# Expert weights as one 8 KB run per partition, with the turned operands taken in steps of two

## What is computed

```python
def _ec_moe(h, w_r, w_g, w_u, w_d):
    ...
    gate, idx = lax.top_k(aff.T, cap)
    xe = t[idx]
    hid = jax.nn.silu(jnp.einsum('ecd,edf->ecf', xe, w_g)) * jnp.einsum('ecd,edf->ecf', xe, w_u)
    ye = jnp.einsum('ecf,efd->ecd', hid, w_d) * gate[..., None].astype(t.dtype)
    out = jnp.zeros_like(t).at[idx.reshape(-1)].add(ye.reshape(-1, d))
```

## Time and profile before

| what | value |
|---|---|
| median of 3 runs | 2408.3 us (2407.99 to 2409.02) |
| span of the profiled execution | 2406.4 us |
| PE busy | 2205.8 us (92%) |
| PE weight loads busy | 1677.9 us (70%) |
| DVE busy | 1613.7 us (67%) |
| ACT busy | 1261.6 us (52%) |
| POOL busy | 545.4 us (23%) |
| DMA | 520.40 MB, 169530 packets |

### The profile page before, as it was taken

One profiled execution on the slowest core, in us unless ns is written; L12 is line 12 of the kernel. 1 busy time (PEld: TensorE's weight loads), 2 busy tenths in 40 slices (PEclk: granted clock), 3 DMA queues, 4 the chain that ended last, 5 costly groups with the idle time before them and its releaser, 6 DMA issues. The chain is left out here.

```text
span 2406.4 us, 32340 instructions
## 1 busy us (share of the span) xinstructions
PE 2205.8 (92%) x11028; PEld 1677.9 (70%) x11028; DVE 1613.7 (67%) x1832; ACT 1261.6 (52%) x1486; POOL 545.4 (23%) x430
## 2 busy tenths in 40 slices
PE   8899998969999999977899999969969999999993
PEld 5677776747777777746788888757756777777772
DVE  3566664578888888855566566552258888888883
ACT  3444443157777777743443434341107777777772
POOL 1100000012234233205232222200000332344222
PEclk9999998979999999987999999989979999999997
DMA  7000004769999999934111112152169999999983
GB/s 264 1 14 8 13 14 156 280 228 378 385 385 378 396 382 383 351 95 135 36 49 49 49 48 61 56 191 88 70 245 342 382 381 389 390 380 383 393 295 126
DMA packets 169530, 520.40 MB, mean 216 GB/s; under 512 B 11808, under 2 KB 49440, under 8 KB 169184
## 3 DMA queue, kind: packets, MB, share of 16 engines
q1 hardware_dynamic: 162272, 494.05, 54.4%
q0 software_dynamic: 7168, 25.17, 4.5%
HBM read 481.43 MB, written 37.75 MB: 216 GB/s over the span
## 5 line engine op out<-in xcount | busy, mean ns | idle before, releaser
L1764 DVE TENSOR_TENSOR m_w_lo<-s_raw,m_w_hi 128x2048 fp32r<-128x2048 f32 x384 | 865.9, 2288 | 144.6 <-ACT m_w_hi L1713 143.0
L1713 ACT ACTIVATE m_w_hi<-s_raw 128x2048 fp32r<-128x2048 f32 x384 | 731.1, 1916 | 175.9 <-PE m_ps_down L1809 77.3
L1807 PE MATMUL m_ps_gate<-m_w_hi,m_xeT_hi 128*96 128x512 f32 x512 | 206.0, 402 | 3.8 <-DVE m_xeT_lo L1770 3.8
L1807 PE MATMUL m_ps_down<-m_w_hi,m_hidT_hi 128*96 128x512 f32 x512 | 203.9, 398 | 3.8 <-DVE m_hidT_lo L1770 3.8
L1809 PE MATMUL m_ps_gate<-m_w_hi,m_xeT_lo 128*96 128x512 f32 x512 | 204.3, 399 | 0.0
L1809 PE MATMUL m_ps_down<-m_w_hi,m_hidT_lo 128*96 128x512 f32 x512 | 204.1, 399 | 0.0
L1807 PE MATMUL m_ps_up<-m_w_hi,m_xeT_hi 128*96 128x512 f32 x512 | 203.9, 398 | 0.0
L1684 POOL DMA_INDIRECT acc<-m_ye,m_row_scatter x32 | 47.0, 1469 | 688.4 <-ACT m_ye L1730 688.4
L1809 PE MATMUL m_ps_up<-m_w_hi,m_xeT_lo 128*96 128x512 f32 x512 | 202.7, 396 | 0.0
L1808 PE MATMUL m_ps_gate<-m_w_lo,m_xeT_hi 128*96 128x512 f32 x512 | 202.5, 395 | 0.0
L1808 PE MATMUL m_ps_down<-m_w_lo,m_hidT_hi 128*96 128x512 f32 x512 | 202.3, 395 | 0.0
(11 more groups left out here) (228 smaller groups left out, 4200.4 us busy)
## 6 DMA issues: line engine op xcount, KB each, us to landing
s_raw<-in_w_gate SPq DMA_DIRECT2D x128, 1024.0 KB, 7.6
s_raw<-in_w_up SPq DMA_DIRECT2D x128, 1024.0 KB, 7.3
s_raw<-in_w_down SPq DMA_DIRECT2D x128, 1024.0 KB, 7.8
s_raw<-in_w_qkv_b SPq DMA_DIRECT2D x16, 512.0 KB, 5.8
s_raw<-in_w_qkv_b SPq DMA_DIRECT2D x32, 256.0 KB, 6.1
s_raw<-in_w_o_b SPq DMA_DIRECT2D x1, 8192.0 KB, 23.2
acc<-o_x SPq DMA_DIRECT2D x12, 512.0 KB, 2.6
xn<-o_xn SPq DMA_DIRECT2D x12, 512.0 KB, 3.0
```

Of the source, the lines that this page charges most:

```text
L1713: act.activation(hi[:, split, :, :].rearrange("p k n -> p (k n)"), raw[:, slot, :], ACT.Copy).then_inc(hi_ready, 1)
L1764: dve.tensor_tensor(lo[:, split, :, :].rearrange("p k n -> p (k n)"), raw[:, slot, :], hi[:, split, :, :].rearrange("p k n -> p (k n)"), A ...
L1807: pe.matmul(out[:, cols], left_hi[:, k, :], hi[:, split, kk, cols], start=(k == 0), stop=False)
```

## The change

The loads read two neighbouring matrix rows into one partition: partition p of piece j now holds rows 256j+2p and 256j+2p+1, which are one run of 8 KB in HBM and in the slot. So that the products still sum over the same rows, each transpose takes its 128 columns in steps of two: block k = 2j+kk of the turned operand holds the columns 256j+2p+kk.

```diff
             def load(e, matrix, j, first_slot):
-                src = matrix[layer].rearrange("e (c k p) n -> e c p k n", c=4, p=P)[bass.ds(e, 1), j]
-                sp.dma_start(raw[:, first_slot + j, :].rearrange("p (k n) -> p k n", k=2),
-                             src.rearrange("e p k n -> (e p) k n")).then_inc(shared.landed[first_slot + j], 16)
+                src = matrix[layer].rearrange("e (c p k) n -> e c p (k n)", c=4, p=P)[bass.ds(e, 1), j]
+                sp.dma_start(raw[:, first_slot + j, :],
+                             src.rearrange("e p n -> (e p) n")).then_inc(shared.landed[first_slot + j], 16)
...
                 wait(pe, T_lo, n)
+                rows = src.rearrange("t (c p k) -> t c k p", c=4, k=2)
                 for k in range(KD):
-                    last = pe.transpose(T_ps[:, k, 0:CAP], src[:, k * P:(k + 1) * P], shared.ident[0:CAP, 0:CAP])
+                    last = pe.transpose(T_ps[:, k, 0:CAP], rows[:, k // 2, k % 2, :], shared.ident[0:CAP, 0:CAP])
...
-        src = matrix[layer, 0].rearrange("(c k p) n -> c p k n", c=4, p=P)
-        sp.dma_start(self.raw[:, first_slot + j, :].rearrange("p (k n) -> p k n", k=2),
-                     src[j]).then_inc(self.landed[first_slot + j], 16)
+        src = matrix[layer, 0].rearrange("(c p k) n -> c p (k n)", c=4, p=P)
+        sp.dma_start(self.raw[:, first_slot + j, :], src[j]).then_inc(self.landed[first_slot + j], 16)
```

## The result

| kernel | median, us | runs from, to | ratio to before, 95% interval |
|---|---|---|---|
| before | 2408.39 | 2407.99 to 2409.02 | |
| changed | 2425.62 | 2423.41 to 2428.76 | 1.0073, 1.0058 to 1.0087 |

The change makes the kernel slower by 17.2 us, clearly more than the 0.2% that a measurement here tells from no change, and by more than the range allowed (it ended at 2423.0). The profiled execution took 2423.4 us, with a span of 2421.3 (2406.4 before). Of all runs in this document one, of the kernel with `hid` alone further down, took 4742.23 us, twice its other nine; it is left out of the ratios, and its cause is not known.

The account below looks back on a forecast made before the run. PE was taken as the full engine, with 34.71 us per expert; loads, gather and scatter, and transposes each counted 0, so 2406.4 us of span + 0 + 1.9 gave 2408.3. The range ran from a little under 2404.0 to 2423.0.

Parts of the forecast that it names:

- its cover of 15.6 us: Gather: lands at about 714.7 us, its rows are turned at 730.25; a doubled landing still early, value 0.
- the count of seven uncovered loads: Turns: the first of eight transpose loads lies beneath the last matmul, so seven count, 64 x 7 = 448.
- Rival B: Products on PE: fewer packets stop disturbing the matmul pitch; a drop by 2 ns would give 2399 us; chance 0.06.
- a third of room: Transposes: the load's estimated 62 ns lies 20 ns under the 82 ns pitch, so a strided read is free until a third slower.
- middle value: Transposes: strided load as long as an ordinary one, 113 ns, costing 448 x 31 ns = 13.9 us.
- rival A: Transposes: strided load outgrows the streamed identity, +13.9 us (2422.2) with ordinary load's time, 18.8 (2427.1) at half rate; chance 0.20.
- the half-rate end: Transposes: strided load at half rate, 124 ns, 42 over the pitch, costing 18.8 us, giving 2427.1 us.

Follow-up runs that it names:

- `hid` alone: Changed kernel, but DVE writes hid in its turn's order, so that turn is contiguous while xe's stays strided: 2415.30 us, ratio 1.0024.
- the version with other rows paired: Kernel before, but the products' stationary operands are read with a step of two, pairing wrong rows: 2406.28 us in one run.

## Why the prediction was wrong

**What held.** PE is the full engine, and what its turns lost shows in the time (16.3 us by the periods, 17.2 by the medians); the loads were ahead everywhere and are worth nothing, neither a gain nor a loss (ratio 0.9998 with the loads alone); 49152 packets went; the gather, slower by 1.4 us, stayed inside its cover of 15.6 us; no new wait came up. The first load of each turn lies beneath a matmul, and the count of seven uncovered loads was right. That the streamed side sets the pitch of contiguous transposes fits its two rows; no run varied it. Rival B, a gain through fewer packets, is refuted by the run with the loads alone.

**The step that failed** is the value taken for the strided transposes. The text put their price between 0 and 18.8 us, took 0, and gave two reasons: the load's part of the pitch was 62 ns by the difference of two durations, with a third of room, and nothing in the trace showed a read that slows for its step. The second was no reason, since no row had such a read at all. The first does not carry: by the same subtraction a load of 217 ns would set a pitch of 113 + 25 = 138 ns and one of 204 ns (step of eight) 125, where 120 and 111 were measured. A difference of durations is not a difference of pitches, and how much room the contiguous load has under 82 ns no run shows. What the runs showed in place of the 0 is a pitch of 0.120 us in the body of a turn with a step of two, 38 ns more than 82. The comparison that should have set the value was in the earlier trace rows: of two loads of 128 columns the transpose's was the quick one, and a step takes what makes it quick. The text priced that as its middle value, with an ordinary load's 113 ns (448 x 31 ns = 13.9 us), and gave rival A, of which it is one end, one chance in five.

**The middle value was itself short by 6 ns a load.** Seven prices show in a turn, as the prediction counted: the second interval is 32 ns longer, the other five 38 each, and the seventh price stands at the end, between the last transpose and the first product. In the kernel before that product, in order of time behind the turn of the earlier trace rows, was

```profile
710.72 0.45 PE L1807 MATMUL m_ps_gate<-m_w_hi,m_xeT_hi 128*96 128x512 f32 x1
```

so it came 710.72 - (710.12 + 0.574) = 0.03 us behind the last transpose; after the change it comes 713.68 - (713.25 + 3 x 0.119) = 0.07 us behind, 0.037 more by the medians over the turns. A turn loses 32 + 5 x 38 + 37 = 259 ns, so 37 for each of the seven, and 64 turns lose 16.6 us, against 16.3 by the periods and 17.2 measured (14 to 21 by the interval). The mean pitch, 32 ns over 82, spreads six of the prices over seven intervals and leaves out the one at the end.

**The range** ended at the middle price and left the half-rate end, 2427.1, outside, although the trace could not choose between them. With the bound that the text itself had worked out, it would have held 2425.6.

**Two rates that the prediction cited.** The Trainium skill, page "SBUF — State Buffer", section "Door 1: The DMA port swizzle", has reads keep full rate with two or more hits in a 16-byte line, which would make a step of two floats free. The runs do not agree for the load of a transpose: with steps of two and four floats alike the pitch rose from 0.082 to 0.120 us, and with eight to 0.111. For the other loads a step of two was nearly free (192 to 196 ns, 163 to 168 ns). The page "TensorE: Matmul & The Clock Gate" of the Trainium skill, section "LDWEIGHTS (loading the stationary operand)", gives 107 ns for 128 columns; the strided transposes (0.111 to 0.120) and the router (0.113) lie 4 to 12% above that, the contiguous transposes with their pitch of 0.082 well below. The rule that the prediction set aside because one row beat it is close to what a step falls back to.

## What to carry to other kernels

Look at the stationary operand of a PE transpose before its layout is changed: with a step it loads at about the ordinary pitch, here 0.11 to 0.12 us for 128 columns instead of at most 0.082, and a row of short transposes has no cover for it; put the step where another engine has room (DVE's reads for `hid` took it for nothing), or beneath a long matmul. Longer runs in a load are worth something only where a wait for a load ends last; here none of ACT's waits was ended by one. Measure a load's price by the start-to-start pitch, interval by interval: a duration overlaps its neighbours, and a mean over a short row mixes covered and uncovered ones. And where no row of the trace has the operation, the value is not the end that seems likeliest: the range goes to both.

## What the runs showed of the hardware

- A row of transposes with 96 streamed columns has a pitch of 82 ns when their load of 128 columns is contiguous, and of 120, 120 and 111 ns with a step of two, four and eight; the load lasts 141, 217, 219 and 204 ns, and 0.20 us with a step of two beneath a matmul. An ordinary load of 128 columns lasts 192 ns contiguous and 196 with a step of two.
- The products became slightly quicker when their stationary operand was read with a step of two: period 34.59 instead of 34.71 us, 0.12 us over 144 matmuls, 0.8 ns each, and much the same (34.56) in the version with other rows paired. Why is open.
- 8 KB runs did not land noticeably sooner than 4 KB runs, 7.8 against 7.9 us for 1 MB of a down piece beside the same traffic, but SP spent 333 instead of 373 ns on issuing one.
